# Differential attention stage: shared score banks, another DVE order, and head norms computed with tokens on partitions

## The reference

```python
q, k, v = jnp.split(h @ w_in, ...)                # 8 heads; q and k: 2 maps of 64, v: 128 wide
q = _rms_norm(q.reshape(bsz, t, 8, 2, 64), g0)    # per token, head and map, over 64 values
k = _rms_norm(k.reshape(bsz, t, 8, 2, 64), g1)
logits = q . k * 64**-0.5 + bias                  # per map; key chunk not later than the query's
p = softmax(logits); pd = p[map 0] - lam * p[map 1]
o = pd @ v                                        # per head, 128 wide
o = _rms_norm(o, subln) * (1 - lambda_init)       # over 128 values
mix = o @ w_out
```

## Time and profile before

| | |
|---|---|
| median of three runs | 4473.8 us |
| the profiled execution, its own time | 4476.38 us |
| its span | 4474.7 us |
| mean granted TensorE clock | 0.928 of full speed |
| PE busy | 3966.1 us, 89% of the span |
| DVE busy | 1530.3 us, 34% |
| ACT busy | 1232.9 us, 28% |
| the stage's loop over heads | from 496.7 to 797 us of the span |
| reciprocal of the head norms (L958) | 8 times, 6753 ns each |
| multiplication of q and k (L961) | 16 times, 936 ns each |

### The profile page before, as it was taken

One profiled execution on the slowest core, in us unless ns is written; L12 is line 12 of the kernel. 1 busy time (PEld: TensorE's weight loads), 2 busy tenths in 40 slices (PEclk: granted clock), 3 DMA queues, 4 the chain that ended last, 5 costly groups with the idle time before them and its releaser, 6 DMA issues. The chain is left out here.

```text
span 4474.7 us, 52766 instructions
## 1 busy us (share of the span) xinstructions
PE 3966.1 (89%) x20908; PEld 3105.6 (69%) x20908; DVE 1530.3 (34%) x2372; ACT 1232.9 (28%) x1735; POOL 228.0 (5%) x217
## 2 busy tenths in 40 slices
PE   7999787799989998588889998999897886798998
PEld 6999666699989995255548876885344563445886
DVE  3222556323233322543323324323672111123332
ACT  3321555233123311233313314421001111102431
POOL 0000311000000000010000000000640000000000
PEclk9999898799999999699999999999898886799999
DMA  3322211122222222000022222221112001112221
GB/s 136 132 83 78 96 43 34 38 85 89 81 74 94 79 80 82 14 26 1 1 76 102 83 77 103 94 87 68 43 52 78 21 0 38 53 64 90 94 89 70
DMA packets 84963, 305.36 MB, mean 68 GB/s; under 512 B 8087, under 2 KB 34839, under 8 KB 66676
## 3 DMA queue, kind: packets, MB, share of 16 engines
q1 hardware_dynamic: 84852, 303.90, 19.4%
HBM read 301.66 MB, written 10.72 MB: 70 GB/s over the span
## 5 line engine op out<-in xcount | busy, mean ns | idle before, releaser
L329 ACT ACT_TABLE_LOAD x60 | 77.0, 1283 | 356.5 <-PE acc L284 356.5
L1738 PE MATMUL acc<-m_xn,s_gw 128*128 128x512 f32 x384 | 171.4, 603 | 0.0
L613 PE MATMUL acc<-a_xh,a_wh 128*128 128x264 f32 x384 | 120.9, 315 | 53.9 <-ACT a_sq L807 37.6
L370 DVE TENSOR_TENSOR fc_wl<-fc_raw,fc_wh 128x2048 fp32r<-128x2048 f32 (+1 forms) x38 | 76.4, 2012 | 244.2 <-ACT fc_wh L329 244.2
L370 DVE TENSOR_TENSOR fa_wl<-fa_raw,fa_wh 128x2048 fp32r<-128x2048 f32 (+1 forms) x38 | 76.4, 2012 | 244.2 <-ACT fa_wh L329 244.2
L370 DVE TENSOR_TENSOR fb_wl<-fb_raw,fb_wh 128x2048 fp32r<-128x2048 f32 (+1 forms) x38 | 76.4, 2012 | 244.2 <-ACT fb_wh L329 244.2
L284 PE MATMUL acc<-fa_xh,fa_wh 128*128 128x264 f32 x704 | 144.9, 287 | 10.8 <-DVE fa_xl L375 10.6
L284 PE MATMUL acc<-fc_xh,fc_wh 128*128 128x264 f32 x704 | 144.8, 287 | 10.9 <-DVE fc_xl L375 10.9
L284 PE MATMUL acc<-fb_xh,fb_wh 128*128 128x264 f32 x704 | 145.1, 287 | 10.4 <-DVE fb_xl L375 10.4
L370 DVE TENSOR_TENSOR fe_wl<-fe_raw,fe_wh 128x2048 fp32r<-128x2048 f32 (+1 forms) x38 | 76.4, 2012 | 220.0 <-ACT fe_wh L329 220.0
L370 DVE TENSOR_TENSOR ff_wl<-ff_raw,ff_wh 128x2048 fp32r<-128x2048 f32 (+1 forms) x38 | 76.4, 2012 | 220.0 <-ACT ff_wh L329 220.0
(11 more groups left out here) (560 smaller groups left out, 9837.8 us busy)
## 6 DMA issues: line engine op xcount, KB each, us to landing
fa_raw<-wi_dram SPq DMA_DIRECT2D x22, 1024.0 KB, 4.8
fb_raw<-wi_dram SPq DMA_DIRECT2D x22, 1024.0 KB, 4.8
fc_raw<-wi_dram SPq DMA_DIRECT2D x22, 1024.0 KB, 4.8
fd_raw<-wi_dram SPq DMA_DIRECT2D x22, 1024.0 KB, 4.8
fe_raw<-wi_dram SPq DMA_DIRECT2D x22, 1024.0 KB, 4.8
ff_raw<-wi_dram SPq DMA_DIRECT2D x22, 1024.0 KB, 4.8
a_raw<-a_qkv_dram SPq DMA_DIRECT2D x24, 512.0 KB, 4.1
s_gw<-gate_w_dram SPq DMA_DIRECT2D x24, 512.0 KB, 3.2
```

The source lines that it names most:

```text
L329: act.activation(wh[:, b, 0:n_], raw[:, b, 0:n_], ACT.Copy).then_inc(rounded, 1)
L370: dve.tensor_tensor(wl[:, b, 0:n_], raw[:, b, 0:n_], wh[:, b, 0:n_].bitcast(F32), ALU.subtract).then_inc(split, 1)
L613: last = pe.matmul(to, x[:, c % RING, ks], part[:, k, a:a + n], start=k == 0 and x is wh and part is xh, stop=k == KC - 1 and x is wl)
L1738: last = pe.matmul(acc[:, GATE_BANK[n % 2], :], gw[:, n % 3, k * P:(k + 1) * P], xn[:, k, :], start=k == 0, stop=k == KC - 1)
```

## The change

`sums` now has the squares as the stationary operand, 128 tokens at a time, and two columns of the block matrix as the moving one. The sums come out with tokens on partitions, 16 columns for the real tokens and 4 for the meta tokens, in a corner of bank 7. Root (ACT) and reciprocal (DVE) work on these 20 columns. A new PE function, `widen`, spreads them back over features: one column of reciprocals, repeated 64 times, is the stationary operand, and the identity is the moving one. It fills banks 4 and 5. `scale_heads` on DVE multiplies q and k by what lies in PSUM.

To free banks 4 and 5, all scores now go to banks 2 and 3 (tiles 1 and 2 side by side), and each scores step waits for the logits of the step before it. `out_sum` moves to bank 4 and to between the halves of the q product. `norm_output(n - 1)` moves on DVE from after the weights of tile 2 to ahead of the logits of tile 1, and `out_root` on ACT to ahead of the q product. The wait on `rooted` before the v product is gone; `widen(n + 1)` stands behind its second half, and `turn(4)` waits for the scaled q and k of head n+1. Not shown: `scores` and `logit` with the new bank and offset, and the names of the new tile and semaphores.

```diff
     META_AT = 400
-    A_BANK, B_BANK = 2, 4
-    T_BANK, O_BANK = 6, 7
-    def score_bank(t):
-        return A_BANK if t % 2 else B_BANK
+    S_BANK, N_BANK, T_BANK, O_BANK = 2, 4, 6, 7
+    def score_at(t):
+        return META + P if t == 2 else 0
...
                     pe.wait_ge(o_sq, 1 + n - 1)
+                    pe.wait_ge(o_root, 1 + n - 1)
                 for s in range(2):
-                    pe.matmul(acc[:, s, :], ones64[:, :], sq[:, s, META:], start=True, stop=True)
-                pe.matmul(acc[:, O_BANK, 256:256 + 2 * META], ones64[:, :], sq[:, :, 0:META],
-                          start=True, stop=True).then_inc(summed, 1)
+                    for j in range(QT):
+                        pe.matmul(acc[:, O_BANK, 320 + 4 * j + 2 * s:322 + 4 * j + 2 * s],
+                                  sq[:, s, META + j * P:META + (j + 1) * P], ones64[:, 0:P:64],
+                                  start=True, stop=True)
+                    last = pe.matmul(acc[0:META, O_BANK, 336 + 2 * s:338 + 2 * s], sq[:, s, 0:META],
+                                     ones64[:, 0:P:64], start=True, stop=True)
+                last.then_inc(summed, 1)
+            def widen(n):
+                pe.wait_ge(r_there, 1 + n + 1)
+                for s in range(2):
+                    for m in range(2):
+                        ms = slice(64 * m, 64 * m + 64)
+                        for j in range(QT):
+                            r_at = 4 * j + 2 * s + m
+                            pe.matmul(acc[ms, N_BANK + s, j * P:(j + 1) * P],
+                                      rs[:, r_at:r_at + 1].to_broadcast([P, 64]), ident[:, :],
+                                      start=True, stop=True)
+                        r_at = 16 + 2 * s + m
+                        last = pe.matmul(acc[ms, O_BANK, 256 + META * s:256 + META * (s + 1)],
+                                         rs[0:META, r_at:r_at + 1].to_broadcast([META, 64]),
+                                         ident[0:META, 0:META], start=True, stop=True)
+                last.then_inc(widened, 1)
...
                 pe.wait_ge(o_sq, 1 + n + 1)
-                pe.wait_ge(pt_there, 1 + step(n, QT))
-                pe.matmul(acc[:, T_BANK, :], ones[:, :], ow[:, 0, META:], start=True,
+                pe.wait_ge(qk_on, 1 + min(n + 2, A_HEADS))
+                pe.matmul(acc[:, N_BANK, :], ones[:, :], ow[:, 0, META:], start=True,
                           stop=True).then_inc(o_sum, 1)
...
             sums(0)
-            pe.wait_ge(rooted, 1 + 1)
             projected(0, 2)
+            widen(0)
             turn_values(0)
...
                     pe.wait_ge(v_nat, 1 + n + 1)
-                    projected(n + 1, 0)
+                    projected(n + 1, 0, (0,))
                 if n:
                     out_sum(n - 1)
+                if ahead:
+                    projected(n + 1, 0, (1,))
                 pe.wait_ge(qk_on, 1 + n + 1)
+                if n:
+                    pe.wait_ge(logits, 1 + step(n - 1, QT))
                 for t in (1, 2):
-                    if n:
-                        pe.wait_ge(logits, 1 + step(n - 1, t + 2))
                     scores(n, t)
...
                     last.then_inc(m_scored, 1)
-                if n:
-                    pe.wait_ge(o_root, 1 + n)
                 turn(n, 1)
-                pe.wait_ge(logits, 1 + step(n, 1))
+                pe.wait_ge(logits, 1 + step(n, 2))
                 scores(n, 3)
...
                 turn(n, 2)
-                pe.wait_ge(logits, 1 + step(n, 2))
+                pe.wait_ge(logits, 1 + step(n, 3))
                 scores(n, 4)
                 if ahead:
-                    pe.wait_ge(rooted, 1 + n + 2)
+                    pe.wait_ge(ev_q, 1 + 2 * (n + 1) + 2)
                     projected(n + 1, 2, (0,))
...
                     projected(n + 1, 2, (1,))
+                    widen(n + 1)
                 else:
...
                     pe.wait_ge(o_sq, 1 + n)
+                if ahead:
+                    pe.wait_ge(qk_on, 1 + n + 2)
                 turn(n, 4)
...
                 act.wait_ge(summed, 1 + n + 1)
-                act.activation(sq[:, :, META:], acc[:, 0:2, :], ACT.Sqrt, scale=1.0 / 64, bias=eps_t[:, :])
-                act.activation(sq[:, :, 0:META], acc[:, O_BANK, 256:256 + 2 * META].rearrange(
-                    "p (s t) -> p s t", s=2), ACT.Sqrt, scale=1.0 / 64, bias=eps_t[:, :]).then_inc(rooted, 1)
+                act.activation(rs[:, 0:16], acc[:, O_BANK, 320:336], ACT.Sqrt, scale=1.0 / 64, bias=eps_t[:, :])
+                act.activation(rs[0:META, 16:20], acc[0:META, O_BANK, 336:340], ACT.Sqrt, scale=1.0 / 64,
+                               bias=eps_t[0:META, :]).then_inc(rooted, 1)
...
                 act.wait_ge(o_sum, 1 + n + 1)
-                act.activation(ow[:, 1, META:], acc[:, T_BANK, :], ACT.Sqrt, scale=1.0 / P,
+                act.activation(ow[:, 1, META:], acc[:, N_BANK, :], ACT.Sqrt, scale=1.0 / P,
                                bias=eps_t[:, :]).then_inc(o_root, 1)
...
                 ahead = n + 1 < A_HEADS
+                if n:
+                    out_root(n - 1)
                 if ahead:
                     take_product(n + 1, 0)
-                if n:
-                    out_root(n - 1)
                 exps(n, 1)
...
                 s, keys, y0 = t % 2, META + t * P, bias_at(t)
-                b = score_bank(t)
+                at0 = score_at(t)
                 lo = META if t == QT else 0
-                dve.wait_ge(scored, 1 + step(n, t))
+                dve.wait_ge(scored, 1 + step(n, max(t, 2)))
                 for m in range(2):
-                    dve.tensor_tensor_reduce(lg[:, s, m, lo:keys], acc[:, b + m, 0:keys - lo],
+                    dve.tensor_tensor_reduce(lg[:, s, m, lo:keys], acc[:, S_BANK + m, at0:at0 + keys - lo],
                                              bias[:, m, n, y0 + lo:y0 + keys], -1.0, 3e38, ALU.add, ALU.min,
...
                         last = dve.tensor_tensor_reduce(
-                            lg[:, 0, m, 0:META], acc[:, b + m, META_AT:META_AT + META],
+                            lg[:, 0, m, 0:META], acc[:, S_BANK + m, META_AT:META_AT + META],
                             bias[:, m, n, y4:y4 + META], -1.0, 3e38, ALU.add, ALU.min, nm4[:, m:m + 1])
...
                 dve.wait_ge(rooted, 1 + n + 1)
-                dve.reciprocal(sq[:, :, :], sq[:, :, :])
-                dve.drain()
+                dve.reciprocal(rs[:, 0:16], rs[:, 0:16])
+                dve.reciprocal(rs[0:META, 16:20], rs[0:META, 16:20]).then_inc(r_there, 1)
+            def scale_heads(n):
+                dve.wait_ge(widened, 1 + n + 1)
                 for s in range(2):
-                    dve.scalar_tensor_tensor(qk[:, n % 2, s, :], qk[:, n % 2, s, :], g_qk[:, s:s + 1],
-                                             sq[:, s, :], ALU.mult, ALU.mult)
+                    dve.scalar_tensor_tensor(qk[:, n % 2, s, META:], qk[:, n % 2, s, META:], g_qk[:, s:s + 1],
+                                             acc[:, N_BANK + s, :], ALU.mult, ALU.mult)
+                    dve.scalar_tensor_tensor(qk[:, n % 2, s, 0:META], qk[:, n % 2, s, 0:META], g_qk[:, s:s + 1],
+                                             acc[:, O_BANK, 256 + META * s:256 + META * (s + 1)],
+                                             ALU.mult, ALU.mult)
                 dve.drain()
...
             norm_heads(0)
+            scale_heads(0)
             dve.wait_ge(x_lo_p, 1 + KC // 2)
...
                 ahead = n + 1 < A_HEADS
+                if n:
+                    norm_output(n - 1)
                 logit(n, 1)
...
                                       ALU.add).then_inc(m_weighed, 1)
-                if n:
-                    norm_output(n - 1)
                 logit(n, 3)
                 weigh(n, 3)
+                if ahead:
+                    norm_heads(n + 1)
                 logit(n, 4)
...
                 if ahead:
-                    norm_heads(n + 1)
+                    scale_heads(n + 1)
             for k in range(A_HEADS - 1):
...
```

More of the change, by code:

```diff
@@ L511, in diff_stage @@
                 sq = sb(st, "a_sq", [P, 2, TOK])
+                rs = sb(st, "a_rs", [P, 20])
                 vt = sb(st, "a_vt", [P, TOK])
@@ L539, in diff_stage @@
                 names = ("c_in c_bw c_dot c_exp c_mask w0 w1 w2 w3 rounded split sq_a sq_d nsum nroot normed x_hi x_lo_d "
-                         "x_lo_p proj_mm ev_q ev_v summed rooted qk_on v_turn v_nat scored logits expd weighed turned "
+                         "x_lo_p proj_mm ev_q ev_v summed rooted r_there widened qk_on v_turn v_nat scored logits expd weighed turned "
                          "pt_there pv_mm o_sq o_sum o_root o_on m_scored m_logits m_expd m_weighed m_turned m_pt m_pv "
@@ L543, in diff_stage @@
                 (c_in, c_bw, c_dot, c_exp, c_mask, w0, w1, w2, w3, rounded, split, sq_a, sq_d, nsum, nroot, normed, x_hi,
```

(8 more changed lines are left out.)

## The result

The changed kernel takes 4509.0 us (median of 4 runs, 4506.6 to 4514.9), the kernel before 4473.2 (4465.3 to 4474.4). The ratio is 1.0086, with a 95% interval from 1.0068 to 1.0103: slower by 36 us, outside the range of the forecast. The profiled execution took 4511.26 us, span 4509.5.

What follows compares the result with a forecast made beforehand. PE's list was taken to bound the stage, with one stop per head set by the chain DVE, ACT, root. Terms of -11.4 us plus 15.8 for the clock gave +4.4: 4478 us in terms of the median, 8-in-10 range 4461 to 4493.

Steps and rivals of the forecast that it cites:

- wait, slow halves, long heads: Around the v product: PE's wait on rooted (37.6 us), its slow first halves (9.2) and two long heads (6.4) go.
- widen, 8 times: On PE behind the v product: 32 wide passes 3.5 us, eight short ones 0.4; 3.9 us a call, 31.2 in all.
- new sums: PE's sums with two moving columns: 1.8 to 2.1 us against 1.96 before, taken as no change.
- stop ahead of turn(4): PE waits until DVE has scaled q and k: 2.1 us a head, 14.7 us in seven heads.
- given back ahead of outputs: From turn(4) to outputs 1.5 us in place of 2.43, ACT's rounding lying under widen: 6.5 us back in seven heads.
- clock: Falls of PE's clock after two thin stretches per head, each expected in every second head: 15.8 us, bounds 0 to 31.6.
- stretch B: From the end of widen to the wide passes of outputs, 4.6 us; a clock fall after it priced at 3.2 us.
- A: Stretch from turn(1) to the end of tile 4's scores, 4.7 us; a clock fall after it priced at 1.32 us.
- Rival 2: Clock falls after both thin stretches in all seven heads: +20.2 us, 4494 us; chance 0.25.
- Rival 4: The stop only moves: PE waits 3.1 us ahead of turn(3) for the root's chain, 22 us, 4500 us; chance 0.05.
- Rival 1: The clock stays at 1.00 through both thin stretches, so the sum is -11.4: 4462 us; chance 0.19.
- Rival 3: In widen, passes on different column halves overlap: 2.0 us in place of 3.9, 15 us less, 4463 us; chance 0.05.

Runs made afterwards that it cites:

- experiment 1: Changed kernel plus eight needless float32 matmuls of 128 columns behind widen(n + 1), in the stop ahead of turn(4): 4481.3 us, ratio 1.0019 to the kernel before.
- experiment 4: Changed kernel's order and banks with the old wide norm; in the last head alone norm_output moved behind the last weights: 4429.2 us, ratio 0.9894.

## Why the prediction was wrong

Its own steps, with the working left out. The work terms can be read in experiment 1, where the clock is 1.00 through the six windows:

```
                                    forecast   measured
wait, slow halves, long heads         -53.2      -53.2
widen, 8 times                        +31.2      +39.8   8 x 4.98
new sums                                0         +2.8   2.24 for 1.96 in 7 heads, 3.1 for 2.1 at first
stop ahead of turn(4)                 +14.7      +14.5
given back ahead of outputs            -6.5       -6.2   1.54 us for 2.43
stop ahead of the k product            +2.4       +2.1
last head                               0         +0.2   34.1 us for 33.9
v product ahead of head 0               0         +2.1   8.28 us for 6.13, low clock
sum without the clock                 -11.4       +2.1   (experiment 1: +7.1, interval +4 to +13)
clock                                 +15.8      +27.7   4509.0 - 4481.3
```

The sum fits the stage: the last `take_output` of experiment 1 starts at 799.65 us of its span, 2.7 us later than in the kernel before (797.00). Another 3.3 us arise behind it, in stages whose code is the same and whose length differs by up to 8 us between the profiles (experiment 4).

The forecast missed by 31 us: 12 of them are the clock, 8.6 `widen`, 4.9 the new sums and the first v product, which stood at nothing, and the rest, near 5 us, lies outside the terms of the stage.

**The step that failed most is the clock**: "expect each in every second head". The fall after stretch B came in all seven heads, and that after A in three. Windows with B alone last 40.7 us against 37.5 with none, so B cost the 3.2 us priced for it. Windows with A as well cost 1.9 to 2.7 us more, not 1.32: the scores of tile 4 run slow too (2.08 for 1.1), and the price counted the slow v half alone. So B's mechanism and price were right, and its frequency was put at half. A's frequency (three of seven) was near, its size was off, and its mechanism isn't shown: filling B removed A's falls as well, and work put into A added some. In place of 15.8 us the runs show 28: against experiment 1 the six windows are 25.9 us longer, what comes ahead of them 1.3 and the last head, into which the fall of head 6 reaches, 1.0. The forecast took the four short heads of the kernel before as a sign that such a stretch often passes, though it had itself measured the new one as 1.1 us longer, with a stop in it. Rival 2, the clock falling twice in each head, was nearest (31.6 us, chance 0.25); its 4494 us lacked the work terms.

**`widen`** was mis-sized by 8.6 us. The wide passes were right (0.109 us each for 0.108). The short ones were taken at 0.05 us each; a pair costs 0.36 us between wide ones, since its passes start 0.203 and 0.078 us behind their predecessors and hold up the next two wide passes. At the end of `widen` eight of them take 0.41 us in all, the 0.05 each of the forecast. Between the wide ones they also keep passes on the two column halves from running side by side.

**Right were**: the removed wait (no L614 behind the root), the reciprocals (0.25 and 0.11 us), the stop of 2.1 us and its cause (four scaling operations on DVE behind the last pass), the give-back, the 0.3 us ahead of the k product, and that `norm_output` is hidden in the full heads. Rival 4 is refuted: `turn(3)` doesn't wait for the chain of the root. Rival 1 (the clock holds) is what experiment 1 made by force, and even then the time is 4481 us, not 4462. Rival 3 was given 0.05; its overlap exists, but not in the changed kernel. Its argument against, the map as the outer loop, costs only 0.6 us (2.57 for 1.97); the 16-row matmuls hinder the rest.

**What the prediction didn't ask** is where the removed wait came from within the change. The order alone gives 28 us, order and banks 44, and the new form of the norm takes all of it back and 35 us more. The wait of 37.6 us had been put down to `norm_output` by the timeline, so a sum per part of the change would have shown that little was left for the new norm to buy: 5.7 - 4.1 = 1.6 us a head, which the banks give as well.

## What to carry to other kernels

When a change removes a wait by two means, price each alone: here the order and the banks were enough, and the second means moved 5 us a head onto the engine that bounds. Where PE's list holds a stop with transposes and 16-row matmuls behind it, count the low clock in every repetition and try filling the stop with needless passes; measure it, as in another place they did no good. Keep short matmuls like the 16-row ones out from between matmuls on half the columns, and let these alternate between the halves.

## What the runs showed that was not expected

- PE multiplying ones through a stop of 2.1 us made the kernel 28 us faster than leaving it idle, at the same length of the stop.
- Needless passes in another place brought nothing back: 4520.6 us for 4509.0, of which they are 6 us and the move of the kernel before 3. The low clock came in more heads, not fewer.
- Passes on different column halves start 0.006 us apart and share 0.109 us; 32 take 1.97 us. One pair of 16-row passes between them undoes this.
- Two-column passes with a new stationary operand of 128 columns start 0.112 us apart in the new sums, the same distance as the needless passes with 128 moving columns in experiment 1. Fewer moving columns bought no time.
